# Stick-breaking attention: the turned weights of both heads leave PSUM in one copy, even blocks by ScalarE, odd blocks by VectorE

## The chip, the cores and the metric

The kernel runs on one NeuronCore of a Trainium2 chip. The metric is the device time of one execution in microseconds. Times are taken in several executions; one more is recorded by the hardware profiler, and its trace is what the rows below come from.

## The reference, cut to what matters

One hybrid encoder layer: a normalised input is projected, one half of the result goes through stick-breaking attention (16 heads of 64, 2048 frames behind 16 learned meta tokens), the other half through a Mamba-2 scan, and an output projection joins both. The change lies in the attention:

```python
z = jnp.einsum("bqhd,bkhd->bhqk", qb, kb).astype(jnp.float32) * scale
strict = s_pos < t_pos
log_keep = jnp.where(strict, jax.nn.log_sigmoid(-z), 0.0)
after = lax.cumsum(log_keep, axis=3, reverse=True) - log_keep
weights = jnp.where(strict, jnp.exp(jax.nn.log_sigmoid(z) + after), 0.0)
outs.append(jnp.einsum("bhqk,bkhd->bqhd", weights.astype(v.dtype), vb))
```

A weight is sigmoid(z) times the product of sigmoid(-z) over all later keys. The kernel makes it as a product that runs along the keys (a scan), not with logarithms.

## The kernel before, in words

The stages run one after the other: norm, features, tokens, scan, attention, output. Attention is the stage from about 1606 to 2598 us of the span. It works through 8 pairs of heads. For each pair there are 4 chunks of 512 queries, and each chunk c has first 5 units on the diagonal (query blocks 0, 1, 2, the narrow tail of meta tokens, and query block 3) and then 4 units of 128 queries by 512 keys for each of the c earlier chunks of keys. That makes 44 units for a pair of heads (20 of them diagonal, 24 full), 352 in all. Every unit holds both heads.

A unit n passes through these steps, each on its own engine, with a ring of buffers and a semaphore between any two:

- TensorE, `scores(n)`: q times k into `a_z` (2 banks, one for each head).
- ScalarE, `sigmoids(n)`: two activations read `a_z`, first `a_keep` = sigmoid(-z), then `a_beta` = sigmoid(z).
- VectorE, `scan(n)`: for each head one scan over `a_keep` into `a_rest`. It waits for `keep_ready` of n. The tail unit has no scan of its own.
- GpSimd, `weigh(n)`: `a_w` = `a_beta` times `a_rest`.

What comes behind it goes by blocks. A block m is 128 keys by the 512 queries of a chunk, there are as many blocks as units, and block m is handled 7 places later (`LAG`), in the turn of unit n = m + 7:

- TensorE, `turn_block(m)`: transposes `a_w` into `a_turn`, 4 for each head in a whole block (8 in all). Blocks on the diagonal are narrower: the five have 8, 8, 6, 4 and 2 transposes, for 512, 512, 384, 256 and 128 queries.
- ScalarE and VectorE, `evacuate`: copy `a_turn` to `a_wt` in SBUF.
- TensorE, `apply(m)`: v times `a_wt` into `a_o`; both heads at once.

No scheduler is at work: every engine takes its instructions in the order in which its loop is written. On TensorE one step is `turn_block(n - 7)`, `apply(n - 8)`, `scores(n + 2)`. On ScalarE it is `sigmoids(n)` and then the copy of block n - 7. On VectorE it is `scan(n)` and then the copy of block n - 7, and at the end of a chunk one product with the gate (`a_out`). `scores(n + 2)` waits for `beta_ready` of unit n.

Before the change each head has its own PSUM bank (`a_turn0`, `a_turn1`) and its own semaphore `turned[h]`. ScalarE copies head 0 of every block as soon as its 4 transposes are done, VectorE copies head 1 of every block after the other 4. There is one `a_turn` of each, so the transposes of head h of block m wait for the copy of head h of block m - 1. The copies are one instruction:

```python
            copy(wt[m % ATS][0:rows, h, first_q:W], turn[h][0:rows, first_q:W]).then_inc(done, 1)
```

Of the kernel before, what the change touches and what calls it, by code (L numbers as in the profile page):

```python
# [24 lines left out]
P = 128  # L25
# [6 lines left out]
W = 512  # L32
# [1009 lines left out]
def attention_stage(nc, scratch):  # L1042
# [71 lines left out]

    PADS = [pads(n) for n in range(N + 1)]

    def on_act(m, h):
        return h == 0

    EVACS = {engine: [sum((on_act(x // 2, x % 2)) == (engine == "act") for x in range(y)) for y in range(2 * N + 1)]  # L1120
             for engine in ("act", "dve")}

    def last_of_chunk(ch):
        return max(n for n in range(ch // NW * U, (ch // NW + 1) * U) if chunk_of(n) == ch)
# [3 lines left out]
    with ExitStack() as ctx:  # L1128
# [14 lines left out]
        ident16 = m_.sbuf("a_ident16", [P, P], BF16)  # L1143
        never = m_.sbuf("a_never", [P, P], BF16)
        z = [m_.psum(f"a_z{r}", [P, 2, W]) for r in range(2)]
        turn = [m_.psum(f"a_turn{h}", [P, W]) for h in range(2)]
        o = m_.psum("a_o", [P, W])
        ones = m_.psum("a_ones", [P, W])

# [4 lines left out]
        stored = m_.sems("a_stored", 2)  # L1154
        z_ready, keep_ready, beta_ready = m_.sem("z_ready"), m_.sem("keep_ready"), m_.sem("beta_ready")
        scanned, w_ready, padded = m_.sem("scanned"), m_.sem("w_ready"), m_.sem("padded")
        turned = m_.sems("a_turned", 2)
        wt_act, wt_dve = m_.sem("wt_act"), m_.sem("wt_dve")
        applied, out_ready = m_.sem("applied"), m_.sem("out_ready")
        m_.start()  # L1160
        block = ctx.enter_context(nc.Block())

        def await_wt(eng, m, h):

            if on_act(m, h):
                eng.wait_ge(wt_act, START + EVACS["act"][2 * m + h + 1])
            else:
                eng.wait_ge(wt_dve, START + EVACS["dve"][2 * m + h + 1])

        @block.sync  # L1170
        def _(sp):
# [56 lines left out]
        @block.tensor  # L1228
        def _(pe):
            def scores(n):  # L1230
                c, k, qi = unit(n)
                pair, ch = n // U, chunk_of(n)
                slot, qb = pair % 2, QB - 1 if qi is None else qi
                if n == 0 or chunk_of(n - 1) != ch:
                    pe.wait_ge(q_loaded[ch % 2], START + 32 * (ch // 2 + 1))
                    if c < 2:
                        pe.wait_ge(k_loaded[slot][c], START + 64 * (pair // 2 + 1))
                if n >= 2:
                    pe.wait_ge(beta_ready, START + n - 1)
                t0 = W * (k + 1) if qi is None else W * k  # L1240
                tn = width(n)
                for h in range(2):
                    for k_part in (k_high, k_low):
                        mm = nc.tensor.matmul(z[n % 2][:, h, 0:tn], q[ch % 2][:, h, qb * P:(qb + 1) * P],  # L1244
                                              k_part[slot][:, h, t0:t0 + tn], start=(k_part is k_high),
                                              stop=(k_part is k_low), skip_group_check=True)
                    if diagonal(n):
                        if qi is None:
                            z_part, never_part = z[n % 2][:, h, 0:META], never[:, P - META:P]
                        else:  # L1250
                            z_part = z[n % 2][:, h, META + qb * P:tn]
                            never_part = never[:, 0:tn - META - qb * P]
                        mm = nc.tensor.matmul(z_part, ident16[:, :], never_part, start=False, stop=True,  # L1253
                                              skip_group_check=True)
                mm.then_inc(z_ready, 1)

            def turn_block(m):
                first, count = GROUP[m]
                _, j, first_q, rows = block_of(m)
                last = first + count - 1  # L1260
                pe.wait_ge(w_ready, START + REAL[last] + 1)
                if diagonal(m):
                    pe.wait_ge(padded, START + PADS[last + 1])
                for h in range(2):
                    if m > 0:
                        await_wt(pe, m - 1, h)
                    for qi in range(first_q // P, QB):
                        tile = w[REAL[member(m, qi)] % AS]
                        x = W + 1 if rows == META else j * P
                        mm = nc.tensor.transpose(turn[h][0:rows, qi * P:(qi + 1) * P], tile[:, h, x:x + rows], ident[:, :])  # L1270
                    mm.then_inc(turned[h], 1)

            def apply(m):
                b, j, first_q, rows = block_of(m)
                pair, ch = m // U, chunk_of(m)
                first = m == 0 or chunk_of(m - 1) != ch
                if first:
                    if ch % NW == 0:
                        pe.wait_ge(v_loaded[pair % 2], START + 32 * (pair // 2 + 1))
                    if ch >= 1:  # L1280
                        pe.wait_ge(out_ready, START + ch)
                for h in range(2):
                    await_wt(pe, m, h)
                for h in range(2):
                    mm = nc.tensor.matmul(o[h * HEAD:(h + 1) * HEAD, first_q:W],  # L1285
                                          v[pair % 2][0:rows, b, h * HEAD:(h + 1) * HEAD], wt[m % ATS][0:rows, h, first_q:W],
                                          start=first, stop=(m == LAST[ch]), skip_group_check=True)
                mm.then_inc(applied, 1)

            pe.wait_ge(made, START + 3)  # L1290
            for n in range(-2, N + LAG + 1):
                if 0 <= n - LAG < N:
                    turn_block(n - LAG)
                if 0 <= n - LAG - 1 < N:
                    apply(n - LAG - 1)
                if 0 <= n + 2 < N:
                    scores(n + 2)

        def evacuate(eng, copy, m, h, done):
            _, _, first_q, rows = block_of(m)  # L1300
            eng.wait_ge(turned[h], START + m + 1)
            if m >= ATS:
                eng.wait_ge(applied, START + m - ATS + 1)
            copy(wt[m % ATS][0:rows, h, first_q:W], turn[h][0:rows, first_q:W]).then_inc(done, 1)  # L1304

        @block.scalar
        def _(act):
            nc.scalar.preload_act_table_set("sigmoid_and_others")
            act.wait_ge(filled, START + 3 + RS + 2 * KEEPS)

            def sigmoids(n):
                tn = width(n)
                lo = W + 1 if is_tail(n) else 0
                act.wait_ge(z_ready, START + n + 1)
                for tile, scale, done in ((keep, -1.0, keep_ready), (beta, 1.0, beta_ready)):
                    if side(n) >= KEEPS:
                        if tile is keep:
                            act.wait_ge(scanned, START + side(n) - KEEPS + 1)
                        else:
                            act.wait_ge(w_ready, START + side(n) - KEEPS + 1)  # L1320
                    nc.scalar.activation(tile[side(n) % KEEPS][:, :, lo:lo + tn], z[n % 2][:, :, 0:tn], ACT.Sigmoid,  # L1321
                                         scale=scale).then_inc(done, 1)

            for n in range(N + LAG):
                if n < N:
                    sigmoids(n)
                if n >= LAG:
                    for h in range(2):
                        if on_act(n - LAG, h):
                            evacuate(act, nc.scalar.copy, n - LAG, h, wt_act)  # L1330

        @block.vector
        def _(dve):
# [28 lines left out]
            for n in range(N + LAG + 2):  # L1362
                if n < N and not is_tail(n):
                    scan(n)
                if 0 <= n - LAG < N:
                    for h in range(2):
                        if not on_act(n - LAG, h):
                            evacuate(dve, nc.vector.tensor_copy, n - LAG, h, wt_dve)
                if n - LAG - 1 in LAST:
                    gated(LAST.index(n - LAG - 1))  # L1370

        @block.gpsimd
        def _(pool):
# [14 lines left out]
            def weigh(n):  # L1388
                r = REAL[n]
                tn = mult_width(n)  # L1390
                if r >= AS:
                    first, count = GROUP[BY_REAL[r - AS]]
                    for h in range(2):
                        pool.wait_ge(turned[h], START + first + count)
                if diagonal(n) and unit(n)[2] < QB - 1:
                    nc.gpsimd.memset(w[r % AS][:, :, tn:tn + P - META], 0.0).then_inc(padded, 1)
                pool.wait_ge(scanned, START + r + 1)
                pool.wait_ge(beta_ready, START + n + 1)
                nc.gpsimd.tensor_tensor(w[r % AS][:, :, 0:tn], beta[r % KEEPS][:, :, 0:tn], rest[r % RS][:, :, 1:tn + 1],  # L1399
                                        ALU.mult).then_inc(w_ready, 1)  # L1400
# [303 lines left out]
```

## Time and profile before

| | us |
|---|---|
| median of 3 runs (3010.36 to 3014.28) | 3011.9 |
| profiled execution, its time | 3010.83 |
| its span | 3009.1 |
| TensorE busy in the span | 2808.2 |
| VectorE busy | 1558.2 |
| ScalarE busy | 1043.3 |
| GpSimd busy | 986.2 |

A line number such as L1304 is one of the kernel before. PE is TensorE's matrix work and PEld its weight loads, DVE is VectorE, ACT is ScalarE, POOL is GpSimd. Matmuls are pipelined, so the busy time of PE counts their overlap as busy; how fast TensorE goes on is read from the starts of its groups. In a timeline each row is a run of equal instructions: start, length in us, engine, line, and in brackets how long the engine had been idle and who released it.

### The profile page before, as it was taken

What the parts mean: (1) busy time and instruction counts of PE and PEld (TensorE: products, weight loads), DVE (VectorE), ACT (ScalarE), POOL (GpSimd) and SP (SyncE); (2) the same over time, 40 slices, a digit from 0 to 9 for tenths busy, and PEclk for the clock granted to TensorE, in tenths of its full rate; (3) what the DMA queues carried; (4) which work ended last, traced back from release to release, by engine and by line L of the source; (5) the groups of instructions that cost most, each with busy time, mean ns of one, the idle gap of its engine ahead of it and who ended that gap; (6) DMA issues with size and microseconds to landing.
All of it is one profiled execution on the core that took longest, in us unless ns stands there. A gap on an engine that the chain in (4) does not pass through costs nothing. (4 is left out here: it accounts for less than half of the span.)

```text
span 3009.1 us, 38715 instructions
## 1 busy us (share of the span) xinstructions
PE 2808.2 (93%) x14210; PEld 2101.1 (70%) x14210; DVE 1558.2 (52%) x1777; ACT 1043.3 (35%) x1502; POOL 986.2 (33%) x694
## 2 busy tenths in 40 slices
PE   4999999999999979979977999999999999689998
PEld 3999999888888848756644555555555555368887
DVE  6112454210000010039965888988889888665554
ACT  4011101111111131111114767767777667432221
POOL 1211211212121100028854655656566555200000
PEclk6999999999999989989987999999999999889999
DMA  3232212232221211125546234143240401252331
GB/s 120 77 132 89 74 63 74 101 135 95 73 73 63 77 75 46 46 63 131 130 120 150 66 76 101 34 113 76 59 113 22 113 22 36 83 160 78 112 98 42
DMA packets 169915, 256.79 MB, mean 85 GB/s; under 512 B 11664, under 2 KB 118416, under 8 KB 162112
## 3 DMA queue, kind: packets, MB, share of 16 engines
q1 hardware_dynamic: 168064, 255.16, 28.8%
q8 instruction: 71, 1.16, 0.2%
q14 instruction: 52, 0.43, 0.0%
q10 hardware_dynamic: 1728, 0.03, 0.0%
HBM read 158.40 MB, written 96.76 MB: 85 GB/s over the span
## 5 line engine op out<-in xcount | busy, mean ns | idle before, releaser
L1399 POOL TENSOR_TENSOR a_w<-a_beta,a_rest 128x1024 f32<-128x1024 f32 (+2 forms) x320 | 560.9, 1753 | 384.0 <-DVE a_rest L1351 352.1
L352 PE MATMUL f_acc<-ut_hi,f_w_hi 128*128 128x512 f32 (+2 forms) x1568 | 582.6, 372 | 14.4 <-POOL f_w_lo L337 14.4
L352 PE MATMUL f_acc<-ut_lo,f_w_hi 128*128 128x512 f32 (+2 forms) x1568 | 584.7, 373 | 0.0
L352 PE MATMUL f_acc<-ut_hi,f_w_lo 128*128 128x512 f32 (+2 forms) x1568 | 583.3, 372 | 0.0
L1351 DVE TENSOR_TENSOR_SCAN a_rest<-a_keep,a_rest,a_ones 128x513 f32<-128x513 f32 x384 | 469.2, 1261 | 0.2
L1270 PE MATMUL a_turn<-a_ident,a_w 128*128 128x128 f32 (+1 forms) x2432 | 342.4, 276 | 24.1 <-DVE a_wt L1304 23.2
L1285 PE MATMUL a_o<-a_wt,a_v 128*64 128x512 f32 (+3 forms) x1408 | 339.4, 560 | 0.0
L1244 PEld LDWEIGHTS a_z<-a_k_high,a_q 128*128 128x128 f32 x704 | 137.2, 195 | 285.5 <-issue 218.0
L334 POOL TENSOR_TENSOR f_w_hi<-f_stage,f_zero 128x1024 fp32r<-128x1024 f32 x44 | 83.4, 1895 | 770.6 <-DMA f_stage<-in_w_blocks 770.6
L1244 PE MATMUL a_z<-a_k_high,a_q 128*128 128x512 f32 (+4 forms) x704 | 297.2, 423 | 39.1 <-DMA a_k_low<-scratch_k_lo 17.5
L352 PEld LDWEIGHTS f_acc<-ut_hi,f_w_hi 128*128 128x128 f32 x1568 | 295.1, 188 | 50.7 <-issue 15.0
L1270 PEld LDWEIGHTS a_turn<-a_ident,a_w 128*128 128x128 f32 (+1 forms) x2432 | 272.4, 140 | 75.6 <-DVE a_wt L1304 43.7
L352 PEld LDWEIGHTS f_acc<-ut_lo,f_w_hi 128*128 128x128 f32 x1568 | 295.2, 188 | 34.7
L352 PEld LDWEIGHTS f_acc<-ut_hi,f_w_lo 128*128 128x128 f32 x1568 | 295.6, 189 | 33.5
L1321 ACT ACTIVATE a_keep<-a_z 128x1024 f32<-128x1024 f32 (+4 forms) x352 | 298.0, 847 | 29.5 <-PE a_z L1253 29.5
L1321 ACT ACTIVATE a_beta<-a_z 128x1024 f32<-128x1024 f32 (+4 forms) x352 | 298.2, 847 | 0.0
L1304 ACT COPY a_wt<-a_turn 128x512 f32<-128x512 f32 (+3 forms) x352 | 185.7, 528 | 295.7 <-PE a_turn L1270 294.4
L1304 DVE COPY a_wt<-a_turn 128x512 f32<-128x512 f32 (+3 forms) x352 | 210.1, 597 | 112.0 <-PE a_turn L1270 111.3
L1244 PE MATMUL a_z<-a_k_low,a_q 128*128 128x512 f32 (+4 forms) x704 | 254.8, 362 | 0.0
L1351 DVE TENSOR_TENSOR_SCAN a_rest<-a_keep,a_ones 128x144 f32<-128x144 f32 (+3 forms) x256 | 203.9, 837 | 52.7 <-ACT a_keep L1321 52.1
L1547 PE MATMUL o_acc<-o_w_hi,o_g_hi 128*128 128x512 f32 x512 | 203.3, 397 | 11.7 <-DVE o_w_lo L1603 7.1
L400 DVE SCALAR_TENSOR_TENSOR f_row_b<-f_acc,f_row_a 128x512 fp32r<-128x512 f32 (+2 forms) x72 | 45.6, 634 | 319.5 <-ACT f_row_a L378 319.5
(170 smaller groups left out, 3447.7 us busy)
## 6 DMA issues: line engine op xcount, KB each, us to landing
f_stage<-in_w_blocks SPq DMA_DIRECT2D x44, 512.0 KB, 5.5
scratch_gate<-f_row_a SPq DMA_DIRECT2D x16, 1024.0 KB, 4.7
o_g<-scratch_mixed SPq DMA_DIRECT2D x32, 512.0 KB, 5.4
scratch_xbc<-f_row_a SPq DMA_DIRECT2D x12, 1032.0 KB, 4.8
s_xc<-scratch_xbc SPq DMA_DIRECT2D x16, 768.0 KB, 5.3
a_k_high<-scratch_k_hi SPq DMA_DIRECT2D x16, 768.0 KB, 12.7
a_k_low<-scratch_k_lo SPq DMA_DIRECT2D x16, 768.0 KB, 18.7
scratch_k_hi<-f_row_a SPq DMA_DIRECT2D x8, 1032.0 KB, 3.9
```

The costliest lines, as they stand in the source:

```text
L334: nc.gpsimd.tensor_tensor(w_hi[s][:, :, :], stage[s][:, :, :], spread(zero[:, :], P).to_broadcast([P, KB, P]), ALU.add).then_inc(w_split[s ...
L352: last = nc.tensor.matmul(acc[c][:, 0:tn], w[s][:, k, :], u[:, k, t0:t0 + tn], start=(k == 0 and u is ut_hi and w is w_hi), stop=(k == KB ...
L400: nc.vector.scalar_tensor_tensor(out=row_b[s][:, cols].bitcast(F32R), in0=acc[c][:, 0:tn], scalar=Q_SCALE if kind == "q" else 1.0, in1=row ...
L1244: mm = nc.tensor.matmul(z[n % 2][:, h, 0:tn], q[ch % 2][:, h, qb * P:(qb + 1) * P], k_part[slot][:, h, t0:t0 + tn], start=(k_part is k_hig ...
L1270: mm = nc.tensor.transpose(turn[h][0:rows, qi * P:(qi + 1) * P], tile[:, h, x:x + rows], ident[:, :])
L1285: mm = nc.tensor.matmul(o[h * HEAD:(h + 1) * HEAD, first_q:W], v[pair % 2][0:rows, b, h * HEAD:(h + 1) * HEAD], wt[m % ATS][0:rows, h, fir ...
L1304: copy(wt[m % ATS][0:rows, h, first_q:W], turn[h][0:rows, first_q:W]).then_inc(done, 1)
L1321: nc.scalar.activation(tile[side(n) % KEEPS][:, :, lo:lo + tn], z[n % 2][:, :, 0:tn], ACT.Sigmoid, scale=scale).then_inc(done, 1)
L1351: mm = nc.vector.tensor_tensor_scan(rest[r % RS][:, h, tn - 1::-1], top, ones[:, 0:1].to_broadcast([P, tn]), start, ALU.mult, ALU.min)
L1399: nc.gpsimd.tensor_tensor(w[r % AS][:, :, 0:tn], beta[r % KEEPS][:, :, 0:tn], rest[r % RS][:, :, 1:tn + 1], ALU.mult).then_inc(w_ready, 1)
L1547: mm = nc.tensor.matmul(acc[n][q][:, :], lhs[s][:, k, :], rhs[:, k, n * W:(n + 1) * W], start=(k == q * KB and lhs is g_hi and rhs is w_hi ...
```

## The change

The two PSUM banks become one tile `a_turn` of 128 x 2 x 512. All transposes of a block, of both heads, count as one: `turned` is one semaphore, raised by the last transpose, and a block's transposes start only when the whole block before it has been copied out. The copy of a block takes both heads in one instruction of twice the elements. Even blocks are copied by ScalarE, odd ones by VectorE. Nothing else moves: the order of scores, sigmoids, scans, products and matmuls on every engine is as before.

```diff
-    def on_act(m, h):
-        return h == 0
+    def on_act(m):
+        return m % 2 == 0
...
-        turn = [m_.psum(f"a_turn{h}", [P, W]) for h in range(2)]
+        turn = m_.psum("a_turn", [P, 2, W])
...
-        turned = m_.sems("a_turned", 2)
+        turned = m_.sem("a_turned")
...
-        def await_wt(eng, m, h):
-
-            if on_act(m, h):
-                eng.wait_ge(wt_act, START + EVACS["act"][2 * m + h + 1])
-            else:
-                eng.wait_ge(wt_dve, START + EVACS["dve"][2 * m + h + 1])
+        def await_wt(eng, m):
+
+            eng.wait_ge(wt_act if on_act(m) else wt_dve, START + m // 2 + 1)
...
+                if m > 0:
+                    await_wt(pe, m - 1)
                 for h in range(2):
-                    if m > 0:
-                        await_wt(pe, m - 1, h)
                     for qi in range(first_q // P, QB):
                         tile = w[REAL[member(m, qi)] % AS]
                         x = W + 1 if rows == META else j * P
-                        mm = nc.tensor.transpose(turn[h][0:rows, qi * P:(qi + 1) * P], tile[:, h, x:x + rows], ident[:, :])
-                    mm.then_inc(turned[h], 1)
+                        mm = nc.tensor.transpose(turn[0:rows, h, qi * P:(qi + 1) * P], tile[:, h, x:x + rows], ident[:, :])
+                mm.then_inc(turned, 1)
...
-        def evacuate(eng, copy, m, h, done):
+        def evacuate(eng, copy, m, done):
             _, _, first_q, rows = block_of(m)
-            eng.wait_ge(turned[h], START + m + 1)
+            eng.wait_ge(turned, START + m + 1)
             if m >= ATS:
                 eng.wait_ge(applied, START + m - ATS + 1)
-            copy(wt[m % ATS][0:rows, h, first_q:W], turn[h][0:rows, first_q:W]).then_inc(done, 1)
+            copy(wt[m % ATS][0:rows, :, first_q:W], turn[0:rows, :, first_q:W]).then_inc(done, 1)
...
-                if n >= LAG:
-                    for h in range(2):
-                        if on_act(n - LAG, h):
-                            evacuate(act, nc.scalar.copy, n - LAG, h, wt_act)
+                if n >= LAG and on_act(n - LAG):
+                    evacuate(act, nc.scalar.copy, n - LAG, wt_act)
...
-                if 0 <= n - LAG < N:
-                    for h in range(2):
-                        if not on_act(n - LAG, h):
-                            evacuate(dve, nc.vector.tensor_copy, n - LAG, h, wt_dve)
+                if 0 <= n - LAG < N and not on_act(n - LAG):
+                    evacuate(dve, nc.vector.tensor_copy, n - LAG, wt_dve)
```

How the rows stand now is seen best in the full units of the last chunk of a pair of heads. In the changed kernel the copy is line 1297, the sigmoids are line 1314, the scans line 1342. On ScalarE before, every unit's two sigmoids are followed by the copy of one head of a block:

```order
L1321 ACTIVATE a_keep<-a_z 128x2x512
L1321 ACTIVATE a_beta<-a_z 128x2x512
L1304 COPY a_wt<-a_turn 128x512
L1321 ACTIVATE a_keep<-a_z 128x2x512
L1321 ACTIVATE a_beta<-a_z 128x2x512
L1304 COPY a_wt<-a_turn 128x512
```

On ScalarE at the same place after the change:

```order
L1297 COPY a_wt<-a_turn 128x1024
L1314 ACTIVATE a_keep<-a_z 128x2x512
L1314 ACTIVATE a_beta<-a_z 128x2x512
L1314 ACTIVATE a_keep<-a_z 128x2x512
L1314 ACTIVATE a_beta<-a_z 128x2x512
L1297 COPY a_wt<-a_turn 128x1024
```

The copy of twice the width stands behind every second pair of sigmoids, in front of the `a_keep` of the next unit; the unit after that has no copy ahead of it.

On VectorE before, in the same units, the two scans of every unit are followed by a copy of one head:

```order
L1351 SCALAR_TENSOR_TENSOR a_rest<-a_keep,a_rest,a_ones 128x513 x2
L1304 COPY a_wt<-a_turn 128x512
L1351 SCALAR_TENSOR_TENSOR a_rest<-a_keep,a_rest,a_ones 128x513 x2
L1304 COPY a_wt<-a_turn 128x512
L1351 SCALAR_TENSOR_TENSOR a_rest<-a_keep,a_rest,a_ones 128x513 x2
```

On VectorE after the change:

```order
L1342 SCALAR_TENSOR_TENSOR a_rest<-a_keep,a_rest,a_ones 128x513 x4
L1297 COPY a_wt<-a_turn 128x1024
L1342 SCALAR_TENSOR_TENSOR a_rest<-a_keep,a_rest,a_ones 128x513 x4
L1297 COPY a_wt<-a_turn 128x1024
L1342 SCALAR_TENSOR_TENSOR a_rest<-a_keep,a_rest,a_ones 128x513 x2
```

Four scans (two units) now stand between two copies. The copy of an odd block m stands behind the scans of unit m + 7, and on ScalarE the `a_keep` of that unit stands behind the copy of the even block m - 1.

## Rows read from the trace of the kernel before

**Rows 1.** Busy time by stretch: attention, and one pair of heads from a restart to its repeat.

```profile
core 0: us, PE busy (x) PEld busy (x) DVE busy (x) ACT busy (x) POOL busy (x), PEclk, DMA share, GB/s
2002.46:2126.05 123.59, 120.61 (x697) 70.75 (x697) 108.01 (x129) 87.83 (x133) 72.70 (x53) 1.00 0.32 78
1606.00:2598.00 992.00, 961.47 (x5513) 564.21 (x5513) 855.62 (x1011) 695.85 (x1042) 574.20 (x406) 0.99 0.28 69
```

**Rows 2.** Timeline of TensorE, one step of a full unit and the next turn.

```profile
2138.49 1.03 PE L1270 MATMUL a_turn<-a_ident,a_w 128*128 128x128 f32 x8
2139.45 1.08 PE L1285 MATMUL a_o<-a_wt,a_v 128*64 128x512 f32 x4
2140.46 0.50 PE L1244 MATMUL a_z<-a_k_high,a_q 128*128 128x512 f32 x1
...
2141.50 1.03 PE L1270 MATMUL a_turn<-a_ident,a_w 128*128 128x128 f32 x8
```

**Rows 3.** Timeline of ScalarE in the same stretch.

```profile
2142.13 0.59 ACT L1304 COPY a_wt<-a_turn 128x512 f32<-128x512 f32 x1 [0.57 <-PE a_turn L1270]
2142.61 1.03 ACT L1321 ACTIVATE a_keep<-a_z 128x1024 f32<-128x1024 f32 x1
```

**Rows 4.** Timeline of VectorE in the same stretch.

```profile
2141.22 2.45 DVE L1351 TENSOR_TENSOR_SCAN a_rest<-a_keep,a_rest,a_ones 128x513 f32<-128x513 f32 x2
2143.58 0.67 DVE L1304 COPY a_wt<-a_turn 128x512 f32<-128x512 f32 x1
2144.16 2.45 DVE L1351 TENSOR_TENSOR_SCAN a_rest<-a_keep,a_rest,a_ones 128x513 f32<-128x513 f32 x2
```

**Rows 5.** Groups by shape: count, busy us, mean ns, idle before.

```profile
L1321 ACT ACTIVATE a_keep<-a_z 128x1024 f32<-128x1024 f32 x224 | 230.7, 1030 | 2.3 <-PE a_z L1253 2.3
L1304 ACT COPY a_wt<-a_turn 128x512 f32<-128x512 f32 x256 | 150.3, 587 | 242.4 <-PE a_turn L1270 242.4
L744 DVE COPY state<-s_ps 128x1024 f32<-128x1024 f32 x1 | 1.2, 1224 | 3.9 <-PE s_ps L723 3.9
L1304 DVE COPY a_wt<-a_turn 128x512 f32<-128x512 f32 x256 | 171.9, 671 | 103.2 <-PE a_turn L1270 102.5
L1304 DVE COPY a_wt<-a_turn 128x256 f32<-128x256 f32 x32 | 13.0, 405 | 6.0 <-PE a_turn L1270 6.0
```

**Rows 6.** Timeline of VectorE: the copy that TensorE waits for in rows 7.

```profile
2125.34 0.65 DVE L1304 COPY a_wt<-a_turn 128x512 f32<-128x512 f32 x1
```

**Rows 7.** Timeline of TensorE where the diagonal units are scored.

```profile
2122.86 1.04 PE L1270 MATMUL a_turn<-a_ident,a_w 128*128 128x128 f32 x8
2123.82 0.43 PE L1285 MATMUL a_o<-a_wt,a_v 16*64 16x128 f32 x4
2124.19 0.33 PE L1244 MATMUL a_z<-a_k_high,a_q 128*128 128x144 f32 x1
...
2124.85 0.61 PE L1270 MATMUL a_turn<-a_ident,a_w 128*128 128x128 f32 x4
2126.05 0.66 PE L1270 MATMUL a_turn<-a_ident,a_w 128*128 128x128 f32 x4 [0.59 <-DVE a_wt L1304]
2126.64 1.08 PE L1285 MATMUL a_o<-a_wt,a_v 128*64 128x512 f32 x4
2127.65 0.39 PE L1244 MATMUL a_z<-a_k_high,a_q 128*128 128x272 f32 x1
...
2128.46 0.50 PE L1270 MATMUL a_turn<-a_ident,a_w 128*128 128x128 f32 x3
...
2133.45 0.28 PE L1244 MATMUL a_z<-a_k_high,a_q 128*128 128x16 f32 x1
...
2134.00 0.38 PE L1270 MATMUL a_turn<-a_ident,a_w 128*16 128x128 f32 x2
2134.31 0.65 PE L1285 MATMUL a_o<-a_wt,a_v 128*64 128x256 f32 x4
2134.89 0.50 PE L1244 MATMUL a_z<-a_k_high,a_q 128*128 128x512 f32 x1
...
2136.12 1.05 PE L1270 MATMUL a_turn<-a_ident,a_w 128*128 128x128 f32 x8
```

**Rows 8.** What TensorE's transposes waited for, whole execution: us, times.

```profile
  DVE a_wt L1304: 66.8, 126
```

More of the change, by code:

```diff
@@ L1115, in attention_stage @@
     PADS = [pads(n) for n in range(N + 1)]
-    def on_act(m, h):
-        return h == 0
-    EVACS = {engine: [sum((on_act(x // 2, x % 2)) == (engine == "act") for x in range(y)) for y in range(2 * N + 1)]
-             for engine in ("act", "dve")}
+    def on_act(m):
+        return m % 2 == 0
     def last_of_chunk(ch):
@@ L1281, in apply @@
                         pe.wait_ge(out_ready, START + ch)
-                for h in range(2):
-                    await_wt(pe, m, h)
+                await_wt(pe, m)
                 for h in range(2):
@@ L1364, in _ @@
                     scan(n)
-                if 0 <= n - LAG < N:
-                    for h in range(2):
-                        if not on_act(n - LAG, h):
-                            evacuate(dve, nc.vector.tensor_copy, n - LAG, h, wt_dve)
+                if 0 <= n - LAG < N and not on_act(n - LAG):
+                    evacuate(dve, nc.vector.tensor_copy, n - LAG, wt_dve)
                 if n - LAG - 1 in LAST:
@@ L1392, in weigh @@
                     first, count = GROUP[BY_REAL[r - AS]]
-                    for h in range(2):
-                        pool.wait_ge(turned[h], START + first + count)
+                    pool.wait_ge(turned, START + first + count)
                 if diagonal(n) and unit(n)[2] < QB - 1:
```

## The prediction, on record before the changed kernel ran

> **What bounds the kernel now.** I read the busy times by stretch first. In attention TensorE is busy for 961 of 992 us, at a granted clock of 0.99, while VectorE has 856, ScalarE 696 and GpSimd 574 [rows 1]. The work repeats by pairs of heads; from one restart to the same restart in the next pair it takes 123.59 us [rows 1], and eight of these make the stage. So I work out one pair of heads and multiply.
>
> Then the timeline of TensorE. For a full unit it goes without a gap: transposes from 2138.49 to 2139.45 (0.96 us), `apply` to 2140.46 (1.01), scores to 2141.50 (1.04), then the next transposes [rows 2]. A step is 3.01 us, two steps are 6.02. VectorE needs 2.94 us for the same step, from one scan pair to the next (2141.22 to 2144.16), [rows 4]. It is nearly as full as TensorE, and only its small lead keeps it out of the way. Who waits for whom says the same: TensorE's transposes (weight loads and matmuls together) waited 66.8 us in 126 places for VectorE's copy [rows 8]. One such wait is seen at 2126.05: the second head's four transposes start 0.59 us late, 0.06 us behind the end of a copy that had stood behind two full scans (2125.34 + 0.65) [rows 6, 7]. There are 11 steps in a pair of heads whose transposes take longer than their number asks for; the excesses over 0.97 us (8 transposes), 0.75 (6), 0.53 (4) and 0.31 (2) sum to 5.0 us (the largest is this one: 2124.85 to 2126.64 is 1.79 against 0.97). TensorE's own work is thus 123.6 - 5.0 = 118.6 us for a pair of heads.
>
> **What the change costs by itself.** The copies get cheaper. A copy of 1024 elements out of PSUM took VectorE 1.22 us where two of 512 take 1.34 [rows 5]. ScalarE shows no such copy; its sigmoid of 1024 elements from PSUM took 1.03 us, two copies of 512 take 1.17 [rows 5]. From below the price is 0.59 (the work of 512), from above 1.17; I take 1.03, the same engine, source and width. VectorE gains 0.12 us and ScalarE 0.14 in two steps. TensorE's instructions stay the same. The Trainium skill, "Perfetto Trace Analysis", section "Optimizing Scalar/DVE Operations", says that grouping work into larger operations helps where the engine is saturated, and also that where ScalarE or VectorE are not saturated but cause bubbles on another engine, breaking instructions up may finish work sooner. By its first half this change is a gain (rival 1), by its second a loss; the rows have to say which holds.
>
> **What it moves: the queues close a loop.** What counts is not the length of a copy but where it stands. Take a full even block m and call t the end of its last transpose. In ScalarE's queue the copy of m stands ahead of `a_keep` of unit m + 8, that stands ahead of the scans of m + 8 on VectorE, those stand ahead of VectorE's copy of block m + 1, and that is what the transposes of m + 2 wait for. One after the other:
>
> - the copy starts 0.03 us behind t: before, the first four transposes start at 2141.50, four of them last 0.61, and ScalarE's copy starts at 2142.13, 0.02 later [rows 2, 3, 7];
> - it lasts 1.03, and the next activation starts 0.11 us ahead of the copy's end (0.59 long, next start 0.48 later) [rows 3]: 0.92;
> - `a_keep` 1.03 [rows 5], and about 0.03 until the scan starts;
> - two scans until the copy behind them starts: 2143.58 - 2141.22 = 2.36, I use 2.37 [rows 4];
> - VectorE's copy 1.22 [rows 5], 0.06 until TensorE goes on [rows 6, 7];
> - eight transposes after a wait: 1.08 (1.03, and four of them took 0.66 after a wait instead of 0.61 [rows 2, 7]).
>
> The sum is 0.03 + 0.92 + 1.03 + 0.03 + 2.37 + 1.22 + 0.06 + 1.08 = 6.74 us for two steps, against 6.02 of TensorE's work. So TensorE stands for 0.72 us in every two full steps, before the transposes of every even block. Before the change the same path was open: ScalarE's copy started 0.40 us ahead of t (2142.13 against 2141.50 + 1.03), lasted 0.48 to the next start, VectorE's took 0.67, and only the second four transposes waited for it (0.66): -0.40 + 0.48 + 1.03 + 0.03 + 2.37 + 0.67 + 0.06 + 0.66 = 4.9 us, well under 6.02, and between the transposes at 2138.49 and 2141.50 there is no gap [rows 2]. The change adds 0.9 us at the head (later start and longer copy) and 1.0 at the tail.
>
> **A pair of heads, summed.** It has 22 such double steps, named here by their even block (0 to 43; blocks 0 to 4, 5 to 9, 14 to 18 and 27 to 31 are the diagonal ones). For each I set the loop, with the sizes that stand in it, against TensorE's own time. TensorE's pieces: transposes of 8 take 0.97 and of 2 take 0.31 (6 and 4 between: 0.75, 0.53), `apply` 1.01 for 512 queries and 0.37 for 128 (0.80, 0.58 between), scores 1.03 full, 0.66 for 144 keys, 0.81 for 272, 0.55 for the tail, 1.23 for the last diagonal unit [rows 2, 7]. Copies scale by rows 5: VectorE 0.94 for 768 elements, 0.67 for 512, 0.41 for 256; ScalarE 0.83, 0.59 and 0.37.
>
> - Blocks 12, 24, 26, 14: full loop, TensorE 6.02 (5.80 for 14, whose loop is shorter too): 4 x 0.72 = 2.9.
> - Blocks 10, 32, 34, 40: the loop is full, but short units are scored, TensorE 5.38 to 5.65: 1.31 + 1.36 + 1.09 + 1.26 = 5.0.
> - Blocks 2, 16, 28, 30: narrow copies, full scans. Block 2: loop 5.33 against 4.71. 0.62 + 0.62 + 0.68 + 0.77 = 2.7.
> - Blocks 4, 18: here VectorE's own chain is longer than the loop. From one copy's end to the next it has four full scans and the copy, 2 x 2.37 + 1.22 - 0.09 = 5.87, and the turns at its ends differ by 0.66 (2 transposes, then 8): 6.53 against 4.58 and 4.36. 1.95 + 2.17 = 4.1.
> - Blocks 8, 38: 0.28 + 0.23 = 0.5.
> - Blocks 0, 6, 20, 22, 36, 42: unit m + 8 is a tail or has a short scan, the loop is 3.3 to 5.2, TensorE 5.2 to 6.2: nothing.
>
> Together 15.2 us of waits for a pair of heads, in place of the 5.0 of before, which are all in steps counted here: 118.6 + 15.2 = 133.8 against 123.6, +10.2. Times 8 is +81.6. Two corrections: in the last pair of heads no units follow, so blocks 38 and 40 do not wait (-1.5), and the first pair has some lower clock, which makes TensorE's own time longer there and hides about 2 us. That leaves +78. The profiled execution took 3010.83 us, 1.7 more than its span, and 1.1 less than the median of the runs, 3011.9. 3011.9 + 78 = 3090.
>
> **Work that I cost at nothing.** The second even-side unit: `a_keep` of m + 9 follows on ScalarE without a copy ahead and is ready near t + 3.9, while VectorE is busy until 5.7. `beta_ready` of m + 8 comes at t + 3.0, the scores that wait for it are due at t + 4.0. GpSimd's product follows a scan that is 1.6 us later than before, but `a_w` is needed three steps later. Each has a microsecond of cover in a full step; in the narrow ones, where TensorE takes 4.4 us for two steps, I find 0.2 to 0.6.
>
> **Rivals.**
> 1. *Faster, chance 4%.* The waits of before go, since VectorE has less to do and every second block needs no copy of it: -5.0 x 8 = -40, 2972 us. It is decided by the loop: that would have to be under 6.02, 0.72 shorter than I sum it. For it speaks that two scans' work plus one copy is 2 x 2.37 + 1.22 - 0.09 = 5.87 us on VectorE, less than TensorE's 6.02. Against it: this load is not a chain, and `a_keep` stands behind ScalarE's copy in its queue.
> 2. *No change, chance 3%.* Between the last transpose of m and the first of m + 1 lie `apply` and scores, 2.05 us [rows 2], and a copy of 1.22 us fits. This is so if each copy could start at once; for ScalarE's it holds, for VectorE's the scans are ahead. 3012 us.
> 3. *Slower, but by half, chance 8%.* ScalarE's wide copy or the hand-overs are shorter, or short waits melt together across double steps: with 0.25 us less in each of the 16 waiting double steps it is -32, 3058 us.
> 4. *Slower by more, chance 10%.* TensorE's granted clock falls where it now pauses. Its share of work in a full double step goes from all to 6.02 / 6.74. A tenth of the stage at the lower of its two levels (1.2 GHz) would cost about 50 us more: 3140. Against it: from 2002.46 to 2126.05, with pauses of 0.6 us in it, the granted clock was 1.00 [rows 1].
> My forecast has 75%.
>
> **How the numbers follow.** What a measurement of this kernel can tell from no change is about 0.2%, 6 us. The likeliest case has 16 waiting double steps x 8 = 128 places, each known to about 0.15 us: 3070 to 3110. To leave no more than 2 in 10 out, the range takes in the near halves of cases 3 and 4: 3058 to 3115. Faster 0.04, same 0.03, slower 0.93.
>
> **What would show it.** In the profile after, the transposes should be released by VectorE's `a_wt` for roughly 120 us in all (15.2 x 8), some 0.7 us in every second full step, and never by ScalarE's. The full double step should be 6.7 us. VectorE should show waits for `a_keep` of about 0.8 us in the scans behind even copies. VectorE's copies of 1024 should take 1.22 us, ScalarE's 1.03. The prediction is wrong if TensorE's two steps stay at 6.0 us, if ScalarE's `a_keep` is ready before VectorE is free, or if the granted clock falls inside the stage.

## The result, and the profile after

The changed kernel takes 3108.6 us (median, 3108.3 to 3110.9), the one before 3011.8 in the same comparison: 97 us more, a ratio of 1.032 (95% interval 1.030 to 1.034). The profiled execution took 3108.7 us, with a span of 3107.0.

First the busy times of the changed kernel by stretch: a pair of heads in which the clock held, one in which it did not, and the 4.4 us of the second in which it fell. The columns are as in [rows 1].

```profile
2156.95:2291.51 134.56, 121.62 (x698) 70.61 (x699) 106.77 (x107) 84.97 (x110) 72.69 (x52) 1.00 0.30 71
2020.83:2156.95 136.12, 123.17 (x698) 71.35 (x699) 106.76 (x107) 84.97 (x110) 72.71 (x52) 0.99 0.29 71
2080.63:2085.03 4.40, 4.40 (x18) 2.23 (x19) 1.89 (x4) 2.06 (x3) 2.29 (x5) 0.66 0.00 0
```

A pair of heads takes 134.56 us, against 123.59 before [rows 1], and 136.12 where the granted clock fell. ScalarE, VectorE and GpSimd all have less or the same work in more time, so none of them is the bound by its load.

Next, what the transposes waited for in the changed kernel (us, times), answering to [rows 8]:

```profile
  issue: 137.0, 119
  DVE a_wt L1297: 101.9, 118
  POOL a_w L1387: 9.6, 9
  ACT a_wt L1297: 0.7, 4
```

There are 118 waits for VectorE's copy and almost none for ScalarE's, though each engine makes half the copies. The "issue" row is the weight loads that belong to the same waits and end them together with the transposes; it is not added to the others. Now the timeline of one double step of full units, blocks 12 to 14, on TensorE, ScalarE and VectorE, weight loads and GpSimd left out:

```profile
2191.52 1.07 PE L1264 MATMUL a_turn<-a_ident,a_w 128*128 128x128 f32 x8 [1.19 <-DVE a_wt L1297]
...
2192.62 1.01 ACT L1297 COPY a_wt<-a_turn 128x1024 f32<-128x1024 f32 x1 [2.05 <-PE a_turn L1264]
...
2193.53 1.03 ACT L1314 ACTIVATE a_keep<-a_z 128x1024 f32<-128x1024 f32 x1
...
2194.56 1.03 PE L1264 MATMUL a_turn<-a_ident,a_w 128*128 128x128 f32 x8
2194.60 2.46 DVE L1342 TENSOR_TENSOR_SCAN a_rest<-a_keep,a_rest,a_ones 128x513 f32<-128x513 f32 x2 [0.86 <-ACT a_keep L1314]
...
2196.97 1.20 DVE L1297 COPY a_wt<-a_turn 128x1024 f32<-128x1024 f32 x1
...
2198.31 1.06 PE L1264 MATMUL a_turn<-a_ident,a_w 128*128 128x128 f32 x8 [0.58 <-DVE a_wt L1297]
```

Read it from top to bottom. But for the transposes of block 13 at 2194.56, which have no wait, each row lets the next one start, by a semaphore or because it stands ahead of it in the same queue: transposes, ScalarE's copy, `a_keep`, the scans (VectorE idle for 0.86 us before them), VectorE's copy, and the transposes of block 14 at 2198.31. From 2191.52 to 2198.31 it is 6.79 us, where two full steps of TensorE take 6.02 [rows 2]. The sizes by shape in the changed kernel, answering to [rows 5]:

```profile
L1297 ACT COPY a_wt<-a_turn 128x1024 f32<-128x1024 f32 x128 | 129.6, 1012 | 310.8 <-PE a_turn L1264 310.8
L1297 DVE COPY a_wt<-a_turn 128x1024 f32<-128x1024 f32 x128 | 154.5, 1207 | 59.1 <-PE a_turn L1264 58.0
```

### The profile page after: what moved, and what is told of

It is laid out like the page before. It is cut to its first block and busy times, and to the rows that moved or that the text cites. A ratio compares the mean times of both kernels' runs of the same rounds, so it can differ in the third digit from the quotient of the medians.

```text
span 3107.0 us, 37376 instructions
## 1 busy us (share of the span) xinstructions
PE 2822.8 (91%) x14210; PEld 2100.4 (68%) x14210; DVE 1548.4 (50%) x1601; ACT 1019.4 (33%) x1326; POOL 985.9 (32%) x694
## 5 line engine op out<-in xcount | busy, mean ns | idle before, releaser
L1264 PE MATMUL a_turn<-a_ident,a_w 128*128 128x128 f32 (+1 forms) x2432 | 329.4, 275 | 103.4 <-DVE a_wt L1297 101.9
L1238 PE MATMUL a_z<-a_k_high,a_q 128*128 128x512 f32 (+4 forms) x704 | 298.9, 425 | 41.2 <-DMA a_k_low<-scratch_k_lo 17.8
L1297 ACT COPY a_wt<-a_turn 128x1024 f32<-128x1024 f32 (+3 forms) x176 | 157.5, 895 | 382.2 <-PE a_turn L1264 382.2
L1297 DVE COPY a_wt<-a_turn 128x1024 f32<-128x1024 f32 (+3 forms) x176 | 186.4, 1059 | 64.0 <-PE a_turn L1264 62.9
```

Of the source, the lines that this page charges most:

```text
L1264: mm = nc.tensor.transpose(turn[0:rows, h, qi * P:(qi + 1) * P], tile[:, h, x:x + rows], ident[:, :])
L1297: copy(wt[m % ATS][0:rows, :, first_q:W], turn[0:rows, :, first_q:W]).then_inc(done, 1)
```

## The experiments

Each was timed together with the kernel before on one chip; they make three groups on three chips, in which the medians of the kernel before were 3011.1, 3011.2 and 3012.8 us. "Waits" are the excess of each step over TensorE's own time for it (the pieces of the prediction), summed over one pair of heads: 5.0 us before, 16.0 after (in the pair without a fall of the clock).

**One joint turn, halves by head.** The kernel before, with only the semaphores joined:

```diff
+                if m > 0:
+                    for h in range(2):
+                        await_wt(pe, m - 1, h)
                 for h in range(2):
-                    if m > 0:
-                        await_wt(pe, m - 1, h)
...
-                    mm.then_inc(turned[h], 1)
+                mm.then_inc(turned[0], 1)
...
-            eng.wait_ge(turned[h], START + m + 1)
+            eng.wait_ge(turned[0], START + m + 1)
...
-                    for h in range(2):
-                        pool.wait_ge(turned[h], START + first + count)
+                    pool.wait_ge(turned[0], START + first + count)
```

> The kernel before (each head's half copied on its own, head 0 by ScalarE, head 1 by VectorE), but the eight transposes count as one: both copies start when all are done, and the next block's transposes wait for both. Queue theory (copy of m ahead of keep of m + 8 on ScalarE, scans, VectorE's copy, transposes): the loop is 0.03 + 0.48 + 1.03 + 0.03 + 2.37 + 0.67 + 0.06 + 1.08 = 5.75 us, under TensorE's 6.02, so no wait in full steps; only the narrow places, where VectorE is late anyway, wait about 0.5 us more each, 11 in a pair of heads: about +40, 3050 us. Rival (the loss is that the one tile is held as a whole, whatever the queues): the wait of about 0.7 us in every second full step is there too, 3090 or more.

Measured: 3036.4 us, ratio 1.008 (1.007 to 1.010). Waits 8.1 us in a pair of heads. Its full double steps (blocks 12 to 14 and 24 to 28) show none over 0.03 us. The joined turn costs 25 us here, around the narrow blocks only. The queue theory stands; the expected cost of the narrow places was 14 us too high.

**Parity exchanged.** In the changed kernel:

```diff
-        return m % 2 == 0
+        return m % 2 == 1
```

> The changed kernel with the engines exchanged: odd blocks by ScalarE, even ones by VectorE. Queue theory: the same loop of 6.74 us in full steps, only the narrow blocks meet it in other places; summed as in the prediction it gives 13.4 us of waits for a pair of heads in place of 15.2, so 14 us less than the changed kernel: about 3094 us. Rival (the loss hangs on which blocks go to which engine, and even blocks on VectorE free the diagonal): under 3060.

Measured: 3088.3 us, ratio 1.026 (1.024 to 1.027). Waits 14.5 us. The full steps wait 0.69 to 0.76 us as before, now ahead of odd blocks. The waits are 1.5 us fewer, 12 us in all, as summed; a further 8 us or so is the clock, which fell once in the stage here, in the last pair of heads behind a pause of 2.47 us, and six times in the changed kernel (every pair of heads but the first and the last took 133.04 to 133.07 us). Which parity goes to which engine moves the loss by a fifth and does not remove it.

**Keep ahead of the copy.** In the changed kernel, on ScalarE alone (`sigmoids` is given a list of which of its two activations to issue):

```diff
+                copies = n >= LAG and on_act(n - LAG)
+                after_copy = n - 1 >= LAG and on_act(n - 1 - LAG)
                 if n < N:
-                    sigmoids(n)
-                if n >= LAG and on_act(n - LAG):
+                    sigmoids(n, (BETA,) if after_copy else (KEEP, BETA))
+                if copies:
+                    if n + 1 < N:
+                        sigmoids(n + 1, (KEEP,))
                     evacuate(act, nc.scalar.copy, n - LAG, wt_act)
```

> The changed kernel, with one thing moved: on ScalarE the first sigmoid (keep) of unit m + 8 goes ahead of the copy of the even block m, its second (beta) stays behind. Queue theory: the loop is cut, the scans of m + 8 follow those of m + 7 at once, full steps take TensorE's 6.02 us; what stays is VectorE's own chain of two full scans and a wide copy (5.87 us) behind narrow blocks, about 6 us of waits in a pair of heads against 5.0 of before: 3010 to 3030 us. Rival (width of the copy or the joint wait costs by itself): the time stays near 3109.

Measured: 3024.0 us, ratio 1.004 (1.003 to 1.006). That is 85 of the 97 us, given back by one change of order, with the same wide copies, the same joint tile and the same engines. Waits 5.5 us. Its timeline on TensorE and VectorE in full steps:

```profile
1937.09 1.03 PE L1264 MATMUL a_turn<-a_ident,a_w 128*128 128x128 f32 x8
...
1938.16 1.23 DVE L1297 COPY a_wt<-a_turn 128x1024 f32<-128x1024 f32 x1
...
1939.31 4.80 DVE L1348 TENSOR_TENSOR_SCAN a_rest<-a_keep,a_rest,a_ones 128x513 f32<-128x513 f32 x4
...
1940.10 1.03 PE L1264 MATMUL a_turn<-a_ident,a_w 128*128 128x128 f32 x8
...
1943.11 1.03 PE L1264 MATMUL a_turn<-a_ident,a_w 128*128 128x128 f32 x8
...
1944.18 1.23 DVE L1297 COPY a_wt<-a_turn 128x1024 f32<-128x1024 f32 x1
```

The scans of two units now run as one stretch of 4.80 us, VectorE's copy starts as soon as the transposes are done, and TensorE's steps are 3.01 us, without a wait. Of the 13 us that this kernel still takes more than the one before, about 8 are not waits: TensorE's clock fell in five of its pairs of heads, each time behind the pause of 1.97 us that stays before the transposes of block 20 (125.6 us for such a pair, 124.0 for the others).

**Alternation with halves.** The kernel before, two tiles and two semaphores, with only the share of the engines changed:

```diff
-        return h == 0
+        return m % 2 == 0
```

> The kernel before with only the alternation: even blocks by ScalarE, odd ones by VectorE, but in two copies of one head each, every head with its own bank and semaphore. Queue theory: the copies start half a block of transposes earlier and the transposes of head 0 need only the first copy; the loop is about 0.03 + 0.48 + 1.03 + 0.03 + 2.37 + 0.67 + 0.06 + 1.10 = 5.8 us, so no wait in full steps, some in narrow ones: 3010 to 3035 us. Rival (giving a whole block to one engine behind the other's queue is what costs): 3080 or more.

Measured: 3049.1 us, ratio 1.013 (1.011 to 1.015), 14 us over the expected range. No wait over 0.14 us in full double steps (12 to 14, 24 to 28), as the loop of 5.8 us says. A pair of heads in which the clock held takes 126.9 us and has 8.3 us of waits, of which 3.4 are before blocks 6 and 20. The clock fell seven times in the stage, once or twice in a pair (128.5 and 129.9 us for the same work). That is about 11 us, which the expectation had at nothing and which is most of the 14. Some of the waits have GpSimd's product as releaser (43 us of weight-load waits in all), which neither theory had.

So neither the joined turn alone (25 us) nor the alternation alone ((8.3 - 5.0) x 8 = 26 us without the clock) makes waits in the full steps; it takes both. No run has both with copies of one head, so what the width adds to the loop is known from the sum and not from a run.

**All copies by ScalarE, wide.** The changed kernel with `on_act` always true and the counts in `await_wt` to match:

```diff
-        return m % 2 == 0
+        return True
```

> The changed kernel with every block copied by ScalarE in one wide copy, none by VectorE; the order on ScalarE is the plain one (keep and beta of n, copy of n - 7). Queue theory: what closes the loop is VectorE's copy behind the scans; without it the scans can run late at no cost. ScalarE's step is 0.92 + 2 x 0.92 = 2.8 us, under TensorE's 3.01, so no wait in full steps; in the narrow ones ScalarE needs 2.1 to 2.5 us where TensorE needs 1.9 to 2.4, 1 to 3 us of waits in a pair of heads in place of 5.0: 2990 to 3005 us, faster than both kernels. Rival (the wide copy that holds the whole tile costs by itself): 3090 or more, since every block now pays it. Second rival (ScalarE becomes the bound): 3030 or more.

Measured: 2979.2 us, ratio 0.989 (0.988 to 0.991): faster than both kernels, and 11 us below the expected range. Waits 0.6 us. The busy times of one pair of heads, columns as in [rows 1]:

```profile
1975.74:2094.82 119.08, 118.94 (x698) 71.06 (x699) 85.63 (x84) 102.33 (x133) 72.69 (x52) 1.00 0.33 81
```

ScalarE is busy 102 of 119 us and is still waited for in next to no place: its transposes' waits for a copy are 2 us in the whole stage. Every block has the wide copy and the joint tile here, and the loss is gone, so neither makes it by itself. (The joined turn did cost 25 us in the first experiment, where VectorE's copy stood behind its scans.)

**Block 19 to ScalarE.** The changed kernel with one odd block of each pair of heads moved, and the counts in `await_wt` to match:

```diff
-        return m % 2 == 0
+        return m % 2 == 0 or m % U == 19
```

> The changed kernel with block 19 of each pair of heads (the first full block behind a narrow one, before which TensorE pauses 2.1 us) also copied by ScalarE. If the short fall of TensorE's granted clock behind block 19, seen in six of the eight pairs, hangs on that pause: the pause goes (2.1 x 8 = 17 us) and the six falls with it (1.56 x 6 = 9 us), 3082 us, and the trace has no stretch of lower clock from 1700 to 2600. Rival (the clock falls by something else): the pause goes but the falls stay or move, 3091 us.

Measured: 3088.4 us, ratio 1.025 (1.024 to 1.027); between the two expectations, 20 us less than the changed kernel. The profile: the step of block 19 waits 0.09 us instead of 2.13, and a pair of heads takes 132.5 us. In two of the eight the clock still fell (134.1 and 133.9 us). Both falls are behind the other long pause, that of block 5, before the transposes of block 6. Busy times of TensorE's product (`apply`) behind the first of them:

```profile
2029.64:2031.38 1.74, 1.74 (x5) 0.29 (x4) 1.22 (x2) 1.63 (x3) 0.67 (x1) 0.56 0.13 42
```

The pause there is 1.75 us long, the product behind it 1.74 us instead of 1.01, at a granted clock of 0.56. The expectation had all six falls of the changed kernel behind block 19. Its trace shows five there and one behind block 5. The five went with block 19's pause; behind block 5's, which stayed, there are two in place of one. So the falls go with the pauses, but not with every pause of that length.

**Keep first, with blocks 5, 19 and 31 to ScalarE.** The kernel of "keep ahead of the copy" with (and the counts in `await_wt` to match):

```diff
-        return m % 2 == 0
+        return m % 2 == 0 or m % U in (5, 19, 31)
```

> The kernel with keep ahead of the copy (e3), with blocks 5, 19 and 31 given to ScalarE too, where VectorE's copy stands behind four full scans and TensorE's steps are short. In e3 these places hold 1.42 + 2.13 + 0.53 + 0.43 = 4.5 of the 5.5 us of waits of a pair of heads. Queue theory: they go, and the falls of the clock behind them: 3024 - 4 x 8 - 8 = 2985 to 2995 us. Rival (the wait moves to ScalarE's beta or to the next copy): no gain, 3015 to 3025.

Measured: 2990.5 us, ratio 0.993 (0.992 to 0.995), as expected. Waits 2.1 us, of which 0.6 are before block 34. No pair of heads between the first and the last is longer than 120.63 us, and the clock fell in none of them.

**Keep first in the kernel before.** The same edit of ScalarE's order, with the copies of one head.

> The kernel before (halves by head) with only the order on ScalarE changed, keep of the next unit ahead of the copy. Queue theory: its loop was 4.9 us and did not bind, its waits are those of VectorE's copy behind full scans, which do not wait for keep there: within 6 us of 3011. Rival (keep first is a gain by itself, so that e3 says nothing of the loop): 2990 or less.

Measured: 3003.6 us, ratio 0.997 (0.996 to 0.998), 7.6 us faster; just past the expected 6. Waits 4.0 us: those of blocks 6 and 18 shrink (0.82 to 0.27, 0.37 to 0.01), the others stay. The order is worth 8 us where its loop does not bind and 85 where it does.

**All copies by ScalarE, in halves.** The kernel before with

```diff
-        return h == 0
+        return True
```

> The kernel before (two tiles, two semaphores, one copy for each head), with all copies by ScalarE and none by VectorE. Queue theory: VectorE's copy behind the scans is gone here too, so the waits are gone, whether the copies are wide or not. ScalarE's step is 2 x 0.48 + 2 x 0.92 = 2.8 us against 2.76 with the wide copy, both under TensorE's 3.01; the narrow places may wait a little more: 2978 to 2990 us. Rival (the wide copy is what gained in the kernel with all copies by ScalarE): 3000 or more.

Measured: 2972.3 us, ratio 0.987 (0.985 to 0.988), the fastest kernel of this study and 6 us below the expected range. Waits 0.35 us; a pair of heads takes 118.8 to 118.9 us, against 119.1 to 119.2 with the wide copy. That two copies of one head serve better than one of both is a small effect: the medians differ by 7 us between two chips, the intervals of the ratios overlap, and in the traces attention from its first transposes to its last is 954.0 us against 956.8. About 3 us are shown; the rest has no cause shown.

## Why the prediction was right

The forecast was 3090 us in a range of 3058 to 3115; 3108.6 came. The mechanism was right, and its size was 19 us too small.

- **The loop.** Summed to 6.74 us for a full double step, measured 6.79. The pieces agree one by one: ScalarE's copy starts 0.03 us behind the transposes, the next activation 0.91 later, `a_keep` 1.03, scans 2.37, VectorE's copy 1.20, and 0.14 until TensorE starts again, where I had 0.06: the one piece that was off by more than 0.02. Keep ahead of the copy cuts just this loop, and the waits of the full steps are gone, while the same order in the kernel before is worth only 8 us. That is shown, not only argued.
- **The sum over a pair of heads.** 15.2 us of waits were forecast in 16 places. Measured in the steps that hold them they are, by even block: 0.66 for block 2 (forecast 0.62), 1.90 for 4 (1.95), 0.31 (0.28), 1.34 (1.31), 0.74 (0.72), 0.75 (0.73), 0.64 (0.62), 2.13 for 18 (2.17), and so on; with 0.03 us more in every turn that follows a wait, 16.0. TensorE's own 118.6 us, which the forecast took from the difference, is borne out by the kernel in which nothing waits (118.8). This term measured 134.56 - 123.59 = 10.97 where I had 10.2: 6 us of the 19.
- **The clock.** This is the largest part of the miss. I had it as a rival with 10%, in place of the forecast; it came on top of it, and small. In six pairs of heads TensorE's granted clock fell to the lower of its levels for 3.4 us, five times behind block 19 and once behind block 5, and a pair took 136.12 or 136.14 instead of 134.56: 6 x 1.56 = 9 us. I had also written that the prediction is wrong if the clock falls inside the stage. By that sign its term for the clock, nothing, was wrong. The number stayed in the range because the falls were short. The evidence that I gave against a fall, pauses of 0.6 us at full clock, said nothing of the pauses of about 2 us that my own sum put before blocks 6 and 20.
- **The corrections at both ends.** I took off 1.5 us for the last pair of heads and 2 us for the first. Neither was there: the last takes 128.46 against 115.95, which is 11.0 without its 1.56 of clock, and the first 143.75 against 132.46, 11.3. That is 3.5 us more than forecast. In the last pair TensorE's steps get shorter too when no scores follow, and the waits grow by as much; I had left that out.

Together 8 x 10.97 + 6 x 1.56 = 87.8 + 9.4 = 97.2, and 97 were measured.

- **The signs.** The transposes were released by VectorE's copy 118 times, 101.9 us in all, where I had roughly 120 in 128 places. That view counts only TensorE's idle time: 0.58 us at 2198.31, where the loop is 0.77 longer than two steps. ScalarE's copy released them 4 times, 0.7 us, where I had said never. VectorE waited 0.86 us for `a_keep` where I had 0.8.
- **The rivals.** "Faster, since VectorE has less to do" fell: VectorE's busy time went down and its copy was waited for longer. "No change, since a copy fits between two turns" holds for ScalarE's copies (0.7 us of waits) and falls for VectorE's. The Trainium skill, "Perfetto Trace Analysis", section "Optimizing Scalar/DVE Operations", says that breaking up instructions may let work be done sooner where ScalarE or VectorE are not saturated but cause bubbles on another engine. The traces agree, but the effect is small: with all copies on ScalarE a pair of heads takes 118.8 to 118.9 us in halves and 119.1 to 119.2 in wide copies. The order of the queue was worth far more (85 us). What it says of saturated engines no run here tests.

What stays open is why the clock fell behind block 19 in five pairs of heads and not in the other three, behind block 5 in one, with the same pause to 0.01 us before it; and why the kernel that alternates in halves waits for GpSimd.

## What to carry to other kernels

A copy out of PSUM is worth what stands behind it in its engine's queue. Before joining or moving one, write down the circle of releases through all queues (here: transposes, ScalarE's copy, keep, scans, VectorE's copy, transposes) and set its length against the bound engine's own time for the same steps; the loads of the engines did not show it here (VectorE was busy for 107 of 134.6 us, ScalarE for 85). If the circle is too long, cut it at its cheapest place: another order on one engine gave back 85 of 97 us, and taking the copies from the engine with the long scans, though that raised ScalarE from 88 us of a pair of heads in the kernel before to 102 (105 in halves), beat that kernel by 1.1 to 1.3%.

## What the runs showed of the hardware

TensorE's clock fell inside attention behind pauses that are shorter than those at its other falls: between 1000 and 2800 us of the changed kernel's span the falls in the other stages and at the start of attention stand behind pauses of 6.0 to 17.8 us, the six later ones in attention behind 1.97 and 1.75 us. The timeline of TensorE in the changed kernel at the pause that waits for the copy of block 19, before the transposes of block 20:

```profile
2078.43 0.23 PE L1247 MATMUL a_z<-a_never,a_ident 128*128 128x128 bf16 x1
2080.63 1.06 PE L1264 MATMUL a_turn<-a_ident,a_w 128*128 128x128 f32 x8 [1.97 <-DVE a_wt L1297]
2081.62 1.61 PE L1278 MATMUL a_o<-a_wt,a_v 128*64 128x512 f32 x4
2083.16 0.70 PE L1238 MATMUL a_z<-a_k_high,a_q 128*128 128x400 f32 x1
...
2085.03 1.25 PE L1264 MATMUL a_turn<-a_ident,a_w 128*128 128x128 f32 x8
```

A pause of 1.97 us, then a product that takes 1.54 us to the next start instead of 1.01, and scores that take 1.87 instead of 1.04. The sixth pair of heads has its fall earlier, at the pause that waits for the copy of block 5:

```profile
2309.40 1.06 PE L1264 MATMUL a_turn<-a_ident,a_w 128*128 128x128 f32 x8 [1.75 <-DVE a_wt L1297]
2310.39 1.69 PE L1278 MATMUL a_o<-a_wt,a_v 128*64 128x512 f32 x4
```

Here is every place of attention behind which the clock fell in a trace, its start left out, and some where it did not, counted over the pairs of heads (the first pair has no pause before block 6 or 7):

| kernel | pause before | its length, us | clock fell behind it |
|---|---|---|---|
| changed | block 20 | 1.97 | 5 of 8 times |
| changed | block 6 | 1.75 | 1 of 7 |
| changed | blocks 12 and 34 | 1.2 | 0 of 16 |
| keep ahead of the copy | block 20 | 1.97 | 5 of 8 |
| block 19 to ScalarE | block 6 | 1.75 | 2 of 7 |
| alternation with halves | block 20 | 1.63 | 5 of 8 |
| alternation with halves | block 6 | 1.40 | 2 of 7 |
| parity exchanged | block 7 | 1.56 | 0 of 7 |
| parity exchanged | block 37, last pair | 2.47 | 1 of 1 |
| joint turn, halves by head | block 6 | 0.76 | 1 of 7 |

Each fall lasted 3.4 us; in the changed kernel it cost about 1.56 us more than the pause itself. The length of the pause alone does not decide: 1.63 us before block 20 was followed by a fall more often than 1.75 before block 6. The same pause of 1.97 us in the same place was followed by one in some pairs of heads and not in others. There is one trace of each kernel, so these counts are of single executions. The other five kernels (all copies by ScalarE in both forms, keep first with blocks 5, 19 and 31 to ScalarE, and the kernel before with and without keep first) have no pause of over 0.9 us there, and their clock fell in no pair of heads but the first, at its start.
